# The last chunk of two feed-forward blocks, computed by halves of the tokens

## The chip, the cores and the metric

The kernel runs on one core of one Trainium2 chip. The metric is the time of one execution on the device in microseconds (us); lower is better. The engines named here: PE is TensorE (matrix products; its weight loads are recorded apart as PEld), DVE is VectorE, ACT is ScalarE, POOL is GpSimd, SP issues the transfers. Every engine runs its own program in order and waits on semaphores that the others raise.

## What is computed

Two transformer-like blocks follow each other on 1024 tokens of width 1024. The change touches the ends of their two feed-forward parts, "f" in the first block and "g" in the second:

```python
    u = causal_dwconv(h @ w_up, dw_w) + dw_b            # f
    gt, v = jnp.split(u, 2, axis=-1)
    return (jax.nn.silu(gt) * v) @ w_down
...
        x = x + gt_f * rmsnorm(y, norm_post_ffn[i])     # end of the first block: x2
...
        h = modulate(rmsnorm_2(x, g_mix_pre[layer]), sh1, sc1)
        proj = h @ w_in[layer]                          # first product of the second block
...
        f = swiglu(hf, w_ffn_gate[layer], w_ffn_up[layer], w_ffn_down[layer])   # g
        x = x + g2 * rmsnorm_2(f, g_ffn_post[layer])
    return x
```

`rmsnorm` divides each token by the root of the mean of its 1024 squares. So the residual sum of a token needs the squares of all its 1024 values of y, and the next norm needs the squares of its residual sum.

## The kernel before

Everything lies transposed: channels on the 128 partitions, in 8 tiles of channels (`ND = 8`), and the 1024 tokens along the free dimension. An fp32 product is made of three passes in fp32r: the weight is split into a high and a low part (`wh` cast by ACT in line 1235, `wl` = raw - wh by DVE in line 1713), the activations likewise, and hi·hi, hi·lo and lo·hi are added in PSUM. A PSUM tile ("acc") is 128 x 1024, two banks of 512 tokens; `product` (line 696, matmuls in line 708) issues for each of the three passes one matmul of 512 tokens for each bank, each with its own weight load.

A feed-forward block has 22 tiles of hidden channels. They are gone through in chunks (`CHUNKS`, one of 2 and five of 4). For every chunk `ffn` makes the up products of its hidden tiles and then 8 down products ("dn", chunk, i), one for each output tile i; DVE adds each to the output y(i) in line 1972 ("yadd"). In the last chunk (`LAST`), the down product of tile i is 4 x 3 x 2 = 24 matmuls. After each yadd of the last chunk ACT squares y(i) (line 1284). In f the squares of tile i go straight to PE as the stationary side of small products with one or two columns (`tile_squares`, line 811) that sum over channels, and DVE multiplies y(i) with the stream x(i) (line 1817) and sums these products in `st` (line 1824). In g DVE sums the squares in `st` (line 1976), and PE sums that over channels (line 787). These column sums stand ahead of the last quarter of the next tile's product.

At the end of f `block_end` runs: ACT takes the root, DVE the reciprocal (line 1779) and five small operations that give the mean square of the new stream without having it (lines 1851 to 1860), a second root and reciprocal follow. PE spreads both reciprocals over the 128 partitions (`spread`, line 796, 8 products of 128 x 128 each). ACT copies the first spread from PSUM to `st` (line 1320). Then DVE walks over the 8 tiles with four operations each, in this order: scaled(i) (line 1876), lower(i-1) (line 1896), summed(i), the residual (line 1882), normed(i) (line 1889); ACT makes the high part of the normed tile (line 1325), DVE the low part (lower). PE consumes each tile at once for three weight tiles of `w_in` abreast (`tiles_abreast`, line 754), 3 x 3 x 2 = 18 matmuls a tile. SP stores the new stream x2.

At the end of g, the end of the program, `residual` is the same without the next norm: DVE scales (line 1917) and adds (line 1922), POOL takes the adds of tiles 1, 3 and 5 (line 2518), and SP stores each tile of 128 x 1024.

The order on each engine is the order in which the program of that engine is written out; nothing is scheduled by a tool. Rings (`Ring`) hand out PSUM tiles, temporaries and weight slots in turn: 4 raw weight slots and 3 split ones.

## Time and profile before

| | us |
|---|---|
| median of 3 runs | 3297.73 |
| lowest and highest run | 3294.17, 3299.56 |
| the profiled execution | 3292.07 |
| its span in the trace | 3290.3 |
| PE busy | 3096.4 (94%) |
| DVE busy | 1712.3 (52%) |
| ACT busy | 1011.6 (31%) |
| TensorE clock granted, mean | 0.962 of full speed |

The profiled execution is one execution apart from the three timed ones. Its span lies 1.8 us inside its own time. Times in the trace run from the span's start: the last chunk of f and the block's end lie at 1319 to 1441 us, those of g at 3211 us to the end. The page gives each group of instructions by line, engine and tile, and what ended the idle time before it; the timeline gives the instructions in order of time, neighbours of one kind merged.

### The profile page before, as it was taken

To read this page: it belongs to the slowest core of one execution; us is meant where nothing else is said; L and a number is where in the kernel's file an instruction comes from. 1 tells how busy PE (TensorE), PEld (TensorE's weight loads), DVE (VectorE), ACT (ScalarE), POOL (GpSimd) and SP (SyncE) were. 2 spreads that over 40 slices of the span, in tenths; PEclk is the share of its full clock that TensorE was granted. 3 is DMA by queue.
4 is the path that set the end of the run, shared out by engine and by line. 5 is a ranking of instruction groups with operands and counts; after the bars stand their busy time and mean duration, and the time that the engine had idled before them with its cause. 6 is when DMAs were issued, how large, how long until landed. Compare 5 with 4: busy or idle time off the path is not lost. (4 is left out here: it accounts for less than half of the span.)

```text
span 3290.3 us, 33491 instructions
## 1 busy us (share of the span) xinstructions
PE 3096.4 (94%) x13786; PEld 2499.5 (76%) x13786; DVE 1712.3 (52%) x1776; ACT 1011.6 (31%) x1203; POOL 399.8 (12%) x161
## 2 busy tenths in 40 slices
PE   7998869899999999989999999899999999999996
PEld 3784357788888888778888877677877788888885
DVE  5697786656556554574511076577455322223225
ACT  3454444332222122233221133476222311111111
POOL 0595550000000000000200034000110000000000
PEclk9998879899999999899999999999998999999998
DMA  6114423132223331321432343531331202112112
GB/s 207 58 33 159 148 96 113 73 109 64 90 77 116 100 100 63 109 77 64 141 113 92 108 154 128 136 74 50 126 118 56 76 26 64 49 38 62 38 45 109
DMA packets 96192, 301.24 MB, mean 92 GB/s; under 512 B 11205, under 2 KB 15045, under 8 KB 95847
## 3 DMA queue, kind: packets, MB, share of 16 engines
q1 hardware_dynamic: 96040, 299.09, 27.8%
q8 instruction: 110, 1.80, 0.2%
q14 instruction: 42, 0.34, 0.0%
HBM read 251.34 MB, written 47.71 MB: 91 GB/s over the span
## 5 line engine op out<-in xcount | busy, mean ns | idle before, releaser
L708 PE MATMUL ps<-mainr,wh 128*128 128x512 f32 (+1 forms) x6592 | 1782.0, 390 | 29.5 <-issue 12.7
L708 PEld LDWEIGHTS ps<-mainr,wh 128*128 128x128 f32 x6592 | 1238.6, 189 | 286.6 <-issue 31.2
L708 PE MATMUL ps<-mainr,wl 128*128 128x512 f32 (+1 forms) x3296 | 1030.7, 389 | 0.0
L708 PEld LDWEIGHTS ps<-mainr,wl 128*128 128x128 f32 x3296 | 623.1, 189 | 128.6
L1713 DVE TENSOR_TENSOR wl<-raw,wh 128x1024 fp32r<-128x1024 f32 (+2 forms) x272 | 294.1, 1083 | 457.1 <-ACT wh L1235 456.9
L1235 ACT CAST wh<-raw 128x1024 fp32r<-128x1024 f32 (+2 forms) x320 | 282.0, 886 | 746.9 <-PE ps L708 538.3
L1972 DVE TENSOR_TENSOR mainf<-mainf,ps 128x1024 f32<-128x1024 f32 x80 | 97.7, 1221 | 215.0 <-PE ps L708 215.0
L754 PE MATMUL ps<-mainr,wh 128*128 128x512 f32 x576 | 164.4, 409 | 36.0 <-issue 21.8
L2013 DVE SCALAR_TENSOR_TENSOR ps<-mainf,vec,ps 128x1024 f32<-128x1024 f32 (+1 forms) x174 | 180.9, 1102 | 2.5 <-ACT ps L1424 2.3
L2497 POOL TENSOR_TENSOR tmp<-tmp,mainf 128x1024 f32<-128x1024 f32 x8 | 27.5, 3444 | 1160.6 <-DMA mainf<-in_rope 1097.5
L1049 PE MATMUL ps<-mainr,wh 128*128 128x512 f32 x512 | 160.3, 395 | 6.3 <-POOL wl L2464 6.1
L2464 POOL TENSOR_TENSOR wl<-raw,wh 128x1024 fp32r<-128x1024 f32 x48 | 114.7, 2400 | 421.3 <-ACT wh L1235 421.3
L754 PEld LDWEIGHTS ps<-mainr,wh 128*128 128x128 f32 x576 | 112.3, 198 | 66.6 <-issue 37.8
L1357 ACT CAST mainr<-tmp 128x1024 fp32r<-128x1024 f32 x44 | 46.2, 1050 | 281.7 <-DVE tmp L1951 215.2
L1936 DVE SCALAR_TENSOR_TENSOR tmp<-ps,vec,tmp 128x1023 f32<-128x1023 f32 x44 | 56.3, 1280 | 137.2 <-ACT tmp L1340 137.1
L1951 DVE TENSOR_TENSOR tmp<-ps,tmp 128x1024 f32<-128x1024 f32 x22 | 26.9, 1225 | 184.7 <-PE ps L708 183.6
L1049 PEld LDWEIGHTS ps<-mainr,wh 128*128 128x128 f32 x512 | 97.0, 190 | 27.5 <-issue 6.9
L2355 DVE TENSOR_REDUCE cols<-ps 128x1 f32<-128x1280 f32 x64 | 95.1, 1487 | 43.6 <-PE ps L1114 43.5
L1114 PE MATMUL ps<-mainr 128*128 128x512 f32 (+1 forms) x384 | 98.4, 396 | 15.4 <-DMA mainr<-sc_k 8.2
L2518 POOL TENSOR_TENSOR mainf<-mainf,mainf 128x1024 f32<-128x1024 f32 x3 | 7.0, 2344 | 864.5 <-DVE mainf L1917 864.5
L1340 ACT ACTIVATE tmp<-ps,vec 128x1024 f32<-128x1024 f32 x44 | 52.9, 1205 | 179.6 <-PE ps L708 179.6
L2477 POOL TENSOR_TENSOR mainf<-mainf,mainf 128x1024 f32<-128x1024 f32 x40 | 100.3, 2506 | 34.1 <-ACT mainf L1436 17.5
(236 smaller groups left out, 2896.8 us busy)
## 6 DMA issues: line engine op xcount, KB each, us to landing
raw<-in_mod_w SPq DMA_DIRECT2D x48, 512.0 KB, 4.5
raw<-in_ada_w SPq DMA_DIRECT2D x48, 512.0 KB, 3.7
raw<-in_f_up SPq DMA_DIRECT2D x44, 512.0 KB, 4.2
raw<-in_g_up SPq DMA_DIRECT2D x44, 512.0 KB, 3.5
raw<-in_w_in SPq DMA_DIRECT2D x40, 512.0 KB, 4.1
raw<-in_pw SPq DMA_DIRECT2D x24, 512.0 KB, 3.6
sc_x<-mainf SPq DMA_DIRECT2D x24, 512.0 KB, 2.6
mainf<-sc_x SPq DMA_DIRECT2D x24, 512.0 KB, 6.2
```

The source lines that it names most:

```text
L708: ins = e.matmul(out, wt[:, a:b], xs[n], start=kk == 0 and t == 0, stop=kk == kt - 1 and t == 2)
L754: ins = e.matmul(out, wt[:, a:b], xs[n], start=kk == 0 and t == 0, stop=kk == kt - 1 and t == 2)
L1049: ins = e.matmul(out, wt[:, a:a + 128], x, start=first and t == 0, stop=last and t == 2)
L1114: ins = e.matmul(k.SC[i][:, a:b], k.q_at[u % 3][:, 128 * qt:128 * qt + 128], k.k_at[u % 3][t][:, a:b], start=t == 0, stop=t == 1)
L1235: e.copy(k.WH(j), k.RAWT(j)).then_inc(*k.to("whi", j))
L1713: e.tensor_tensor(k.WL(j), k.RAWT(j), k.WH(j).bitcast(F32), ALU.subtract).then_inc(*k.to("wlo_dve", j))
L1936: e.scalar_tensor_tensor(out=t[:, 1:T], in0=ps[:, 0:T - 1], scalar=k.V("fdw", 3 * f + 1), in1=t[:, 1:T], op0=ALU.mult, op1=ALU.add).then_i ...
L1972: e.tensor_tensor(y(i), y(i), k.ACC(s + "_dn", c, i), ALU.add).then_inc(*k.to("yadd", s, c, i))
L2013: e.scalar_tensor_tensor(out=out[:, a:b], in0=k.U(i)[:, tap + a:tap + b], scalar=k.V("dww", TAPS * i + tap), in1=k.CVP(i)[:, a:b], op0=ALU ...
L2355: e.tensor_reduce(k.STAT(n, i), k.SC[i], AX.X, ALU.max, negate=True).then_inc(*k.to("atmax", n, i))
L2464: e.tensor_tensor(k.WL(j), k.RAWT(j), k.WH(j).bitcast(F32), ALU.subtract).then_inc(*k.to("wlo_pool", j))
L2477: e.tensor_tensor(k.CV(i), k.CV(i), k.PROD(added), ALU.add).then_inc(*k.to("gadd", i, tap))
```

## The change

The last chunk leaves `ffn` and gets a sequence of its own, `last_steps`, which all engines follow. Each down product of the last chunk is now made for 512 tokens at a time, h = 0 or 1: ("dn", i, h) is 12 matmuls into one PSUM bank. The order is (0,0), (0,1), (1,0), (1,1), then half 0 of tiles 2 to 7, then half 1 of tiles 2 to 7. The down weights of two tiles form one weight tile ("dp", p) of 1024 columns. The column sums, the root and reciprocal ("cols"), the spread of the first reciprocal ("res"), of the second ("norm", f alone) and the walk ("pass", i, h) are steps of that sequence for each half. All operations of the walk are 512 tokens wide. In f the first pass stands behind "cols" of half 1; in g passes stand between the last products. In f `scaled` now always reads the copy in `st`, which ACT makes in its step "res". POOL's adds in g go to DVE, the output is stored by halves, and the root's table load on ACT moves ahead of the last chunk. In f x2 is stored when half 1 of a tile is done.

```diff
-        for i in range(ND):
+        for i in range(ND if c < LAST else 0):
             yield ("dn", c, i)
+def last_steps(s):
+    first = [("dn", i, h) for i in range(2) for h in range(2)] + [("dn", i, 0) for i in range(2, ND)]
+    if s == "f":
+        return (first + [("dn", 2, 1), ("dn", 3, 1), ("cols", 0), ("dn", 4, 1), ("res", 0), ("dn", 5, 1), ("norm", 0),
+                         ("dn", 6, 1), ("dn", 7, 1), ("cols", 1), ("pass", 0, 0), ("res", 1), ("pass", 1, 0), ("norm", 1)]
+                + [("pass", i, 0) for i in range(2, ND)] + [("pass", i, 1) for i in range(ND)])
+    return (first + [("dn", 2, 1), ("dn", 3, 1), ("cols", 0), ("dn", 4, 1), ("res", 0), ("dn", 5, 1), ("pass", 0, 0),
+                     ("dn", 6, 1), ("pass", 1, 0), ("pass", 2, 0), ("dn", 7, 1), ("pass", 3, 0), ("pass", 4, 0), ("cols", 1),
+                     ("pass", 5, 0), ("res", 1), ("pass", 6, 0), ("pass", 7, 0)] + [("pass", i, 1) for i in range(ND)])
+def half_before(s, i, h):
+    halves = [step[1:] for step in last_steps(s) if step[0] == "dn"]
+    n = halves.index((i, h))
+    return halves[n - 1] if n else None
...
+    def half_ahead(self, s, i, h):
+        key = {(0, 0): (s + "_dp", 2), (2, 0): (s + "_dp", 3)}.get((i, h))
+        if s in NEXT and (i, h) in ((4, 1), (6, 1)):
+            key = NEXT[s][1][i // 2 - 2]
+        return self.W[key] + 1 if key else 0
...
+        w.wait_ge(*k.at("xyadd", s, ND - 2, h))
+        half_columns(k.S(1)[:, 512 * h:512 * h + 512], k.YC(h, 8), 1, m.ones[:, 0:1], False, False, "x" + s, 0, h)
+        w.wait_ge(*k.at("xy", s, ND - 1, h))
+        half_columns(k.TMP("xy", s, ND - 1, h), k.YC(h, 8), 1, m.ones[:, 0:1], False, False, "x" + s, 1, h)
+        half_squares(s, ND - 1, h)
...
+    def last_chunk(s, slots, lo_hi=None):
+        fs = CHUNKS[LAST]
+        for step in last_steps(s):
+            what, h = step[0], step[-1]
+            a, b = 512 * h, 512 * h + 512
+            if what == "dn":
+                i = step[1]
+                j = k.W[s + "_dp", i // 2]
+                before = half_before(s, i, h)
+                hold_weight(j)
+                hold_half(s + "_dn", i, h)
+                x = lambda kk: ([k.R(slots[0][fs[kk] % 5])[:, a:b]], [k.R(slots[1][fs[kk] % 5])[:, a:b]])
+                sums = s == "f" and before and before[0] < ND - 1
+                product(j, len(fs), x, lambda kk: [("uhi", s, fs[kk]), ("ulo", s, fs[kk])], [k.HALF(s + "_dn", i, h)],
+                        512 * (i % 2), (lambda: half_squares(s, *before)) if sums else None).then_inc(*k.to(*k.half_tile(s, i, h)))
+            elif what == "cols":
+                half_sums(s, h)
+            elif what == "res":
+                hold_half("res", s, h)
+                half_spread("y" + s, h, k.HALF("res", s, h), k.COL("rs", 0, 8))
+            elif what == "norm":
+                n = NEXT[s][0]
+                hold_aux("spread", n, h, banks=(h,))
+                half_spread(n, h, aux[:, a:b], k.COL("rn", 0, 8))
...
+                n, keys = NEXT[s]
+                kk = step[1]
+                w.wait_ge(*k.at("prehi", n, kk, h))
+                w.wait_ge(*k.at("prelo", n, kk, h))
...
+    def last_chunk(s, out, acc_free, hi=None, shift=None, after=()):
+        n = NEXT[s][0] if s in NEXT else None
+        e.activation(k.COL("dum", ("f", "g").index(s)), m.eps[RMS_EPS], ACT.Sqrt)
+        for step in last_steps(s):
+            what, h = step[0], step[-1]
+            a, b = 512 * h, 512 * h + 512
+            if what == "dn":
+                i = step[1]
+                split_to(k.half_ahead(s, i, h))
+                w.wait_ge(*k.at("yadd", s, LAST, i, h))
...
+                e.activation(dst, out(i)[:, a:b], ACT.Square).then_inc(*k.to("ysq", s, i, h))
+            elif what == "cols":
+                if n and h:
+                    split_to(k.W[NEXT[s][1][2]] + 1)
...
+                e.activation(k.COL("rs", 4 * h, 4), src, ACT.Sqrt, bias=m.eps[RMS_EPS]).then_inc(*k.to("sqrt", "y" + s, h))
+            elif what == "res" and n:
+                w.wait_ge(*k.at("stat", s, 4, h))
+                e.activation(k.COL("rn", 4 * h, 4), k.COL("xx", 4 * h, 4), ACT.Sqrt, bias=m.eps[RMS_EPS]).then_inc(*k.to("sqrt", n, h))
+                w.wait_ge(*k.at("spread", "y" + s, h))
+                for event in acc_free:
+                    w.wait_ge(*k.at(*event))
+                e.copy(k.S(0)[:, a:b], k.HALF("res", s, h)).then_inc(*k.to("rcopy", s, h))
+            elif what == "pass" and n:
+                i = step[1]
+                w.wait_ge(*k.at("premul", n, i, h))
...
+                e.activation(hi(i)[:, a:b], k.TMP("pre", n, i, h)[:, 0:512], ACT.Identity, bias=shift(i)).then_inc(*k.to("prehi", n, i, h))
+        if n:
+            split_to(k.W[NEXT[s][1][2]] + 2)
...
+            elif what == "res" and n:
+                rn = k.COL("rn", 4 * h, 4)
+                w.wait_ge(*k.at("sqrt", n, h))
+                e.reciprocal(rn, rn).then_inc(*k.to("rec", n, h))
+            elif what == "pass":
+                i = step[1]
+                xs = x(i)[:, a:b]
+                scaled(i, h, a, b)
+                if n and i:
+                    lower(i - 1, h, a, b)
+                w.wait_ge(*k.at("rmul", s, i, h))
+                w.wait_ge(*k.at(f"x{i}", x_load))
+                e.tensor_tensor(xs, xs, y(i)[:, a:b], ALU.add).then_inc(*k.to("res", s, i, h))
+                if n:
...
+                    hold_tmp("pre", n, i, h)
+                    e.scalar_tensor_tensor(out=k.TMP("pre", n, i, h)[:, 0:512], in0=xs, scalar=k.COL("gm", i), in1=aux[:, a:b],
+                                           op0=ALU.mult, op1=ALU.mult).then_inc(*k.to("premul", n, i, h))
+                    if i == ND - 1:
+                        lower(i, h, a, b)
...
-    for i in (1, 3, 5):
-        w.wait_ge(*k.at("rmul", "g", i))
-        w.wait_ge(*k.at(f"x{i}", "x3"))
-        e.tensor_tensor(k.F(10 + i), k.F(10 + i), k.F(i), ALU.add).then_inc(*k.to("resp", "g", i))
...
+    def last_chunk(s, load, x, key):
+        w.wait_ge(*k.at("tile", k.W[s + "_up", FF - 1, 1]))
+        for p in range(ND // 2):
+            feed(k.W[s + "_dp", p] + RAW)
+            load(2 * p)
+            load(2 * p + 1)
+        if s in NEXT:
+            feed(k.W[NEXT[s][1][2]] + 1 + RAW)
+        for step in last_steps(s):
+            if step[0] != "pass" or (s in NEXT and step[2] == 0):
+                continue
+            _, i, h = step
+            w.wait_ge(*k.at("res", s, i, h))
+            channel(f"st{i}")
+            if s in NEXT:
+                e.dma_start(d[key][i], x(i)).then_inc(*k.land(f"st{i}", key))
+            else:
+                a, b = 512 * h, 512 * h + 512
+                e.dma_start(d[key][i][:, a:b], x(i)[:, a:b]).then_inc(*k.land(f"st{i}", key, h))
```

What now stands in a row on ACT at the end of f (`st<-ps` is the copy of the first spread, `mainr<-tmp` the high part of a normed tile, `wh<-raw` the cast of the third `w_in` weight tile, `cols` the roots). Before:

```order
L1235 CAST wh<-raw 128x1024 [waits s_tile,s_raw2]
L1260 ACTIVATE cols<-ps,cols 128x8 [waits s_cols]
L1316 ACTIVATE cols<-cols 128x8 [waits s_ends_dve]
L1320 COPY st<-ps 128x1024 [waits s_rmul]
L1325 ACTIVATE mainr_24576_51<-tmp,cols 128x1024 [waits s_premul] x8
```

and of the changed kernel, half 1:

```order
L1361 CAST wh<-raw 128x1024 [waits s_tile,s_raw2]
L1516 ACTIVATE cols<-ps,cols 128x4 [waits s_cols]
L1529 ACTIVATE mainr_24576_51<-tmp,cols 128x512 [waits s_premul]
L1519 ACTIVATE cols<-cols 128x4 [waits s_ends_dve]
L1523 COPY st<-ps 128x512 [waits s_spread]
L1529 ACTIVATE mainr_24576_51<-tmp,cols 128x512 [waits s_premul] x15
```

The high part of the first normed half tile now stands ahead of the second root and of the copy of half 1, and the other fifteen behind them.

PE at the same place, behind the last column sums. Before (line 796 the two spreads, 754 the products with `w_in`):

```order
L796 MATMUL ps<-ident,cols 128x128 [waits s_rec,s_yadd]
L796 MATMUL ps<-ident,cols 128x128 x7
L796 MATMUL ps<-ident,cols 128x128 [waits s_ends_dve,s_rec,s_sqrt]
L796 MATMUL ps<-ident,cols 128x128 x7
L754 MATMUL ps<-mainr_24576_51,wh 128x512 [waits s_wlo_dve,s_whi,s_yadd,s_prelo,s_prehi]
```

and of the changed kernel (line 1025 the products with `w_in`, 917 a spread of half 1):

```order
L1025 MATMUL ps<-mainr_24576_51,wh 128x512 [waits s_wlo_dve,s_whi,s_yadd,s_prelo,s_prehi]
L1025 MATMUL ps<-mainr_8192_61,wh 128x512
L1025 MATMUL ps<-mainr_24576_51,wl 128x512
L1025 MATMUL ps<-mainr_24576_51,wh 128x512 [waits s_yadd,s_wlo_dve,s_whi]
L1025 MATMUL ps<-mainr_8192_61,wh 128x512
L1025 MATMUL ps<-mainr_24576_51,wl 128x512
L1025 MATMUL ps<-mainr_24576_51,wh 128x512 [waits s_wlo_dve,s_whi]
L1025 MATMUL ps<-mainr_8192_61,wh 128x512
L1025 MATMUL ps<-mainr_24576_51,wl 128x512
L917 MATMUL ps<-ident,cols 128x128 [waits s_rec]
L917 MATMUL ps<-ident,cols 128x128 x3
L1025 MATMUL ps<-mainr_24576_51,wh 128x512 [waits s_prelo,s_prehi]
```

The spread that ACT's copy waits for now stands behind nine products that need the first normed half tile.

DVE at the end of g of the changed kernel, from the add of the sixth tile's second half (line 2104 yadd, 2110 the sum of squares, 2085 scaled, 2160 the residual, 2133 the reciprocal):

```order
L2104 TENSOR_TENSOR mainf_8192_57<-mainf_8192_57,ps 128x512 [waits s_tile]
L2110 TENSOR_TENSOR st<-st,tmp 128x512 [waits s_yacc,s_ysq]
L2085 SCALAR_TENSOR_TENSOR mainf_8192_57<-mainf_8192_57,cols,ps 128x512 [waits s_spread,s_gain,s_yadd]
L2160 TENSOR_TENSOR mainf_16384_58<-mainf_16384_58,mainf_8192_57 128x512 [waits s_x0,s_rmul]
L2104 TENSOR_TENSOR mainf_8192_57<-mainf_8192_57,ps 128x512 [waits s_tile]
L2110 TENSOR_TENSOR st<-st,tmp 128x512 [waits s_yacc,s_ysq]
L2085 SCALAR_TENSOR_TENSOR mainf_8192_57<-mainf_8192_57,cols,ps 128x512 [waits s_yadd]
L2160 TENSOR_TENSOR mainf_16384_58<-mainf_16384_58,mainf_8192_57 128x512 [waits s_x1,s_rmul]
L2085 SCALAR_TENSOR_TENSOR mainf_8192_57<-mainf_8192_57,cols,ps 128x512 [waits s_yadd]
L2160 TENSOR_TENSOR mainf_16384_58<-mainf_16384_58,mainf_8192_57 128x512 [waits s_x2,s_rmul]
L2104 TENSOR_TENSOR mainf_8192_57<-mainf_8192_57,ps 128x512 [waits s_tile]
```

Five of the sixteen passes stand ahead of the reciprocal of half 1, three of these ahead of the last yadd; two more stand between that reciprocal's spread and the passes of half 1.

## Rows read from the trace of the kernel before

**Rows 1.** The page, part 1: busy us, share of the span, instructions.

```profile
PE 3096.4 (94%) x13786; PEld 2499.5 (76%) x13786; DVE 1712.3 (52%) x1776; ACT 1011.6 (31%) x1203; POOL 399.8 (12%) x161
```

**Rows 2.** Timeline of PE, first tile of f's last chunk: start, us, what [idle <-releaser].

```profile
1326.81 1.25 PE L708 MATMUL ps<-mainr,wh 128*128 128x512 f32 x4 [3.61 <-DVE mainr L1960]
1333.97 1.84 PE L811 MATMUL ps<-cols,tmp 128*128 128x2 f32 x16
```

**Rows 3.** Timeline of PE, end of f, from the last down product on.

```profile
1382.20 0.90 PE L708 MATMUL ps<-mainr,wl 128*128 128x512 f32 x2
1385.51 3.57 PE L811 MATMUL ps<-cols,tmp 128*128 128x2 f32 x16 [2.40 <-ACT tmp L1284]
1392.35 5.56 PE L796 MATMUL ps<-ident,cols 128*128 128x128 f32 x32
1402.61 1.84 PE L754 MATMUL ps<-mainr,wh 128*128 128x512 f32 x4 [4.70 <-issue]
```

**Rows 4.** Timeline of DVE, end of f: the two reciprocals and the walk.

```profile
1389.41 0.20 DVE L1779 RECIPROCAL cols<-cols 128x8 f32<-128x8 f32 x1 [0.26 <-ACT cols L1260]
...
1393.75 0.20 DVE L1779 RECIPROCAL cols<-cols 128x8 f32<-128x8 f32 x1 [0.37 <-ACT cols L1316]
1396.15 1.28 DVE L1876 SCALAR_TENSOR_TENSOR mainf<-mainf,cols,ps 128x1024 f32<-128x1024 f32 x1 [2.20 <-PE ps L796]
...
1401.22 1.28 DVE L1896 SCALAR_TENSOR_TENSOR mainr<-tmp,cols,mainr 128x1024 fp32r<-128x1024 f32 x1
...
1403.68 1.28 DVE L1889 SCALAR_TENSOR_TENSOR tmp<-mainf,cols,ps 128x1024 f32<-128x1024 f32 x1
...
1406.18 1.28 DVE L1896 SCALAR_TENSOR_TENSOR mainr<-tmp,cols,mainr 128x1024 fp32r<-128x1024 f32 x1
...
1435.93 1.28 DVE L1896 SCALAR_TENSOR_TENSOR mainr<-tmp,cols,mainr 128x1024 fp32r<-128x1024 f32 x1 [1.22 <-ACT mainr L1325]
```

**Rows 5.** Timeline of ACT: a high part, and the first work behind the walk.

```profile
1404.99 1.15 ACT L1325 ACTIVATE mainr<-tmp,cols 128x1024 fp32r<-128x1024 f32 x1 [3.81 <-DVE tmp L1889]
...
1439.08 1.05 ACT L1235 CAST wh<-raw 128x1024 fp32r<-128x1024 f32 x1 [3.18 <-PE ps L754]
```

**Rows 6.** Groups by form, 512 tokens wide: busy us, mean ns of one.

```profile
L2013 DVE SCALAR_TENSOR_TENSOR ps<-mainf,vec,ps 128x512 f32<-128x512 f32 x58 | 38.5, 748 | 2.3 <-ACT ps L1424 2.3
L2077 DVE TENSOR_TENSOR tmp<-tmp,ps 128x512 f32<-128x512 f32 x16 | 10.9, 680 | 15.3 <-ACT tmp L1390 15.0 <-DMA sc_H<-tmp 0.3
L1235 ACT CAST wh<-raw 128x512 fp32r<-128x512 f32 x96 | 58.9, 618 | 257.0 <-PE ps L708 252.6 <-PE ps L1049 4.4
```

**Rows 7.** A window: us, busy of PE, PEld, DVE, ACT, POOL, granted clock, DMA share, GB/s.

```profile
2035.00:2040.00 5.00, 3.28 (x19) 2.40 (x18) 1.29 (x2) 2.27 (x4) 2.37 (x1) 1.00 0.00 0
```

**Rows 8.** Timeline of PE, end of g.

```profile
3252.13 1.07 PE L708 MATMUL ps<-mainr,wh 128*128 128x512 f32 x4
...
3253.49 1.84 PE L787 MATMUL ps<-ones,st 128*128 128x1 f32 x16
...
3256.22 0.62 PE L708 MATMUL ps<-mainr,wl 128*128 128x512 f32 x2
3259.24 3.19 PE L787 MATMUL ps<-ones,tmp 128*128 128x1 f32 x16 [2.40 <-ACT tmp L1284]
```

**Rows 9.** Timeline of DVE, end of g.

```profile
3266.80 1.28 DVE L1917 SCALAR_TENSOR_TENSOR mainf<-mainf,cols,ps 128x1024 f32<-128x1024 f32 x1 [3.83 <-PE ps L796]
...
3269.26 2.47 DVE L1917 SCALAR_TENSOR_TENSOR mainf<-mainf,cols,ps 128x1024 f32<-128x1024 f32 x2
...
3284.66 1.22 DVE L1922 TENSOR_TENSOR mainf<-mainf,mainf 128x1024 f32<-128x1024 f32 x1
```

**Rows 10.** Timeline of DVE, the last hidden tile of g.

```profile
3211.60 1.23 DVE L1951 TENSOR_TENSOR tmp<-ps,tmp 128x1024 f32<-128x1024 f32 x1 [9.55 <-PE ps L708]
3213.95 1.23 DVE L1960 TENSOR_TENSOR mainr<-tmp,mainr 128x1024 fp32r<-128x1024 f32 x1 [1.12 <-ACT mainr L1357]
```

**Rows 11.** The page, part 6: x count, KB each, median us to landing.

```profile
out<-mainf SPq DMA_DIRECT2D x8, 512.0 KB, 2.6
```

309 lines of the change are left out of this document (209 added, 100 removed).

## The prediction

> **What bounds the kernel now.** The page comes first: PE is busy for 94% of the span and DVE for 52% [rows 1], so over most of the span PE sets the pace, and a change can pay only where PE waits. I then went to the timelines of PE and DVE at the two places that the change touches.
>
> At the end of f the last down product ends at 1382.20 + 0.90 = 1383.10, and the first product with w_in starts at 1402.61 [rows 3]. Between them PE only makes column sums and spreads, with gaps of 2.40 and 4.70 us. DVE starts its walk over the 8 tiles at 1396.15, 13.05 us behind the last product, and ends it at 1435.93 + 1.28 = 1437.21, after 41.06 us [rows 4]. One tile takes 1406.18 - 1401.22 = 4.96 us there. PE needs only 18 matmuls for a tile. Six matmuls take 3253.49 - 3252.13 = 1.36 us [rows 8], 0.227 us each, so 4.08 us a tile: DVE sets the pace of the walk. The next work hangs on the first w_in tile, which ACT picks up at 1439.08 [rows 5].
>
> At the end of g nothing follows. The last product ends at 3256.22 + 0.62 = 3256.84 [rows 8], DVE's last add at 3284.66 + 1.22 = 3285.88 [rows 9]; then comes the last store.
>
> **The end of f, from its start.** What goes away is the wait of half 0 for the sums of half 1. I count four terms: until the last down product, from there to the walk, the walk, and what hangs on it.
>
> First term, PE until the last down product. The last chunk's first tile needs the last hidden tile only for its fourth quarter, and PE already waits 3.61 us for it [rows 2]. Before, 18 matmuls (4.08 us) of that tile cover the wait. Now the first product has 12 matmuls, nine ahead of that quarter (2.04 us), so the wait grows by 2.04 us. The 192 matmuls of the chunk stay 192, each already with its own weight load. Column sums of a whole tile are 16 records in 1.84 us [rows 2], 0.115 each; of a half 8 in 0.92. The squares cost the same in sum. Before, one set of 1.84 (the stream's products) stood ahead of the last product's end; now three sets for half 0 do, 2.76: +0.92. Two spreads of half 0, 8 records each, come between the products too: at 0.12 each 0.96, at the mean of the 32 before (5.56 us, [rows 3]) 1.39. I take the first, since PE is busy there and the 32 began behind a gap: +1.92 (to +2.8). Sum +4.9: the last product ends at 1388.0.
>
> Second term. DVE adds 512 tokens in 0.68 us and multiplies them with the stream in 0.75 [rows 6]: with the hand-overs 1.54. PE sums that product (0.92, at 2.5) and the squares (at 3.4). The root takes 0.3, the reciprocal 0.2 [rows 4], the five small operations I take like it, 1.0 together. The walk can start 5.0 us behind the last product, not 13.05: -8.05. It no longer waits for a spread, since half 0's were made long before. The cast and the low part of the third w_in weight (1.05 on ACT [rows 5] and about 1.2 on DVE) lie beside the column sums. If PE runs at the low clock there, where 16 records took 3.57 us [rows 3], 1.8 us come on top; its gap is now only 0.6 us, so I take none.
>
> Third term, the walk itself. None of its 16 passes stands ahead of the last product: the first is behind "cols" of half 1. So the walk is not beside the products at all in f, it only begins earlier, and it is made of twice as many instructions. A half saves 0.53 us (1.28 against 0.748, 1.22 against 0.680, [rows 4, 6]), not half of it. From lower to lower DVE needs 1403.68 - 1401.22 = 2.46 to normed, less two times 0.53, 1.40; normed 0.75; then ACT's high part, 1.15 [rows 5] less what the cast saves (1.05 - 0.618 = 0.43, [rows 5, 6]), 0.72; hand-overs 0.07. That is 2.94 us a pass, 15 times from the first lower to the last, 44.1. With 3.07 ahead of the first, 0.77 for the last and 0.8 for the change of halves (the high part of tile 7 has nothing beside it) the walk is 48.75 us against 41.06: +7.7.
>
> On top come two waits that the order makes. ACT and PE go through "pass (0,0)" ahead of "res (1)". DVE ends normed(0) 2.3 us into the walk, at 7.3 behind the last product. ACT makes the high part (8.0), then the second root (8.3), for which DVE waits with its reciprocal ahead of pass (1,0): about 1.0 lost. Then lower(0) ends at 9.8. PE makes the nine products of pass (0,0) first. It has waited 6 us by then; behind a gap of 4.70 four matmuls took 1.84 [rows 3], and nine at 0.43 take 3.9, until 13.7. The spread follows, 0.96 to 1.8 (14.7 to 15.5), ACT's copy 0.6, and only then ACT makes the high part of tile 1 (16.1 to 16.9), which lower(1) needs, 12.0 without this. DVE waits 4.4 us. If PE were at full speed at once, nine take 2.04 and the wait is 2.2. Queued behind ACT's waiting copy are fifteen high parts, behind PE's spread all products with w_in. I take 5.4 for both waits, bounds 3.2 and 6.4.
>
> Fourth term. Behind the last lower the first w_in tile needs three matmuls, not six: -0.7. PE then waits for what ACT and DVE make of it, as before. SP stores x2 only with half 1, issued as the tiles are done, and the last store follows the last add as it did; its readers come more than 10 us later. SP's loads of the stream stand ahead of the down products and stay early. These I cost at nothing.
>
> The sum for f: 4.9 - 8.05 + 7.7 + 5.4 - 0.7 = **+9.25 us**, bounds +6 and +13.
>
> **The end of g.** The low part of the last hidden tile is ready at 3213.95 + 1.23 = 3215.2, the down products start as DVE's line 1951 does, at 3211.6 [rows 10]. Before, the fourth quarter is reached at 3215.7, without a wait; now at 3213.6: +1.6. The column sums inside the products stay 1.84, a spread of 0.96 is added: the last product ends at 3259.4 (a wait that short leaves the clock up: in the window 2035 to 2040, PE busy 3.28 of 5 us, it stayed at 1.00 [rows 7]).
>
> On DVE a half product costs yadd 0.68, the wait for ACT's square (0.62, as the cast of [rows 6]) and the sum 0.68: 2.1 with hand-overs, inside the 2.72 of PE. A pass is scaled and add: 3269.26 - 3266.80 = 2.46 [rows 9] less 1.07, 1.39. From the end of product (5,1), 5.44 ahead of the last: 2.1 and one pass, yadd (6,1) starts at 3.4 where its product ended at 2.7; 2.1 and two passes, yadd (7,1) at 8.2 instead of 5.5. From here DVE is the bound. Two passes cover the square, the column sums and the root of half 1 (11.6), the reciprocal 0.2, eleven passes 15.3: 27.2, or 21.8 behind the last product, 3281.2. POOL's three adds are now in these passes; before they saved DVE 3 x 1.14. Against 3285.88 that is **-4.7 us**. The last store, 2.6 us for 512 KB [rows 11], may be some tenths shorter with half the bytes; I take none. Bounds: -6 with that and a shorter first wait, -2.5 if the clock falls for the first products as it did in f.
>
> **Sum.** +9.25 - 4.7 = +4.6 us. The profiled execution took 3292.07, 1.8 over its span, and lies 5.7 under the median; I add the sum to the median: 3297.73 + 4.6 = **3302.3**. What a measurement here can tell from no change is about 0.2%, 6.6 us: 3291.1 to 3304.3.
>
> **The rivals.**
>
> *The low clock in the walk (slower).* PE gets 9 matmuls (2.04 us) for every 2.94 us of DVE. If the clock once fallen stays at 1.2 GHz, nine take 3.9, PE becomes the bound of the walk: 15 x 0.95 = 14.3 more, 3316.6. It decides as soon as nine matmuls need over 2.94. Against it: the window of [rows 7] held 1.00 at a busy share of 66% with gaps, and at low clock the nine fill PE wholly, the state in which it has risen elsewhere. The Trainium skill, "TensorE: Matmul & The Clock Gate", section "HAM oscillation — how this bites in real kernels", describes a kernel whose bursts of matmuls were shorter than the waits between them and which started every burst at the low clock; by that rule this rival would need waits longer than the bursts, and they are shorter here. Chance 0.12.
>
> *Halves at half price (faster, a little).* If a pass of 512 took half of 4.96, 2.48, f would save 7.4 and g's thirteen passes 2: 3292.9. Against it stand the rows of 512-wide operations. Chance 0.08.
>
> *The change does what its name says in f.* If DVE made half 0's passes beside the products of half 1, some 23 us of the walk would be hidden: about 3279. The order of DVE excludes it, the first pass is behind the second "cols". Chance 0.04.
>
> *Something else waits*, such as a ring slot or a weight among the halves, 3 us or more in either block: 3306 and up. Chance 0.08.
>
> **How the numbers follow.** The forecast has 0.68, its own range 3297 to 3308, since its bounds add to -0.5 to +10 and its waits are the soft terms; some 0.50 of it lie under 3304.3, 0.18 above. Faster by over 0.2%: 0.04 of the third and 0.03 of the second rival, 0.07. Slower: 0.18 + 0.12 + 0.06 = 0.36. Within: 0.57. The range runs from the second rival to beyond the fourth, 3293 to 3312.
>
> **What would show it.** In f: PE's wait ahead of the first tile's last quarter near 5.6 us; the first scaled 5 us behind the last product; one lower of DVE waiting 4 us for ACT, and ACT's copy waiting for a spread behind nine slow matmuls; lowers 2.94 apart; the walk over 50 us long. In g: a wait of 1.6 in the first product, no idle DVE from yadd (6,1) on, the last add 22 us behind the last product. It would be wrong if PE's clock stays at 0.50 through the walk, if lowers stand 2.5 apart, or if DVE idles between passes in g.

## The result

The changed kernel takes 3301.3 us (median of 17 runs, 3293.6 to 3309.4), the kernel before 3294.5 us (17 runs, 3287.7 to 3300.4). The ratio is 1.0021, 95% interval 1.0015 to 1.0028: slower by 5 to 9 us, some 7 at the middle. The forecast was 3302.3 us, 4.6 us above the median that it started from.

The profiled execution took 3307.02 us with a span of 3305.2, 14.9 us more than the profiled one of before. Part 1 of the page of the changed kernel:

```profile
PE 3105.4 (94%) x13786; PEld 2500.9 (76%) x13786; DVE 1724.8 (52%) x1863; ACT 1017.2 (31%) x1223; POOL 392.8 (12%) x158
```

Against [rows 1] PE has 9.0 us more and DVE 12.5; the shares are the same. The 14.9 us can't all be the change. To see where they lie I took five events that both programs have and compared the stretches between them: DVE's multiply of f's last hidden tile, ACT's cast behind the walk [rows 5], a table load of ACT in the second block, DVE's multiply of g's last hidden tile [rows 10], DVE's last add [rows 9]. Timelines of the kernel before, DVE and ACT, the two events that no row ahead has:

```profile
1323.10 1.23 DVE L1946 TENSOR_TENSOR tmp<-tmp 128x1024 f32<-128x1024 f32 x1
...
2081.33 1.28 ACT L1645 ACT_TABLE_LOAD   x1
```

The five events in the changed kernel, timelines of DVE and ACT:

```profile
1329.44 1.23 DVE L2195 TENSOR_TENSOR tmp<-tmp 128x1024 f32<-128x1024 f32 x1
...
1454.87 1.05 ACT L1361 CAST wh<-raw 128x1024 fp32r<-128x1024 f32 x1 [1.95 <-PE ps L1025]
...
2097.80 1.28 ACT L1810 ACT_TABLE_LOAD   x1
...
3231.53 1.23 DVE L2200 TENSOR_TENSOR tmp<-ps,tmp 128x1024 f32<-128x1024 f32 x1 [8.59 <-PE ps L771]
...
3300.77 0.69 DVE L2160 TENSOR_TENSOR mainf<-mainf,mainf 128x512 f32<-128x512 f32 x1
```

| stretch, us | before | after | difference |
|---|---|---|---|
| start to f's last hidden tile | 1323.10 | 1329.44 | +6.34 |
| **f**: from there to the cast behind the walk | 115.98 | 125.43 | **+9.45** |
| to the table load | 642.25 | 642.93 | +0.68 |
| to g's last hidden tile | 1130.27 | 1133.73 | +3.46 |
| **g**: from there to the end of the last add | 74.28 | 69.93 | **-4.35** |
| to the span's end | 4.42 | 3.74 | -0.68 |

The change touches the f and g stretches and the last store: +9.45 - 4.35 - 0.68 = +4.4 us, where the prediction's sum was +4.55. The other 10.5 us stand where both programs issue the same; the same kernel run again (e9) shows that these differ between executions. The lower end of the measured interval is +4.9 us, above these +4.4. Where the rest lies is not shown: over all kernels below, the stretch behind the walk alone comes out between 640.0 and 643.0 us, so its +0.68 can't be told from chance.

**f, the first product.** Timeline of PE of the changed kernel (start, us, what, idle before and releaser):

```profile
1324.85 0.61 PE L771 MATMUL ps<-mainr,wl 128*128 128x512 f32 x2
1329.55 1.19 PE L771 MATMUL ps<-mainr,wh 128*128 128x512 f32 x2 [4.09 <-issue]
```

and of DVE, the read of the last up tile and the low part of the hidden tile:

```profile
1328.06 1.28 DVE L2188 SCALAR_TENSOR_TENSOR tmp<-ps,vec,tmp 128x1022 f32<-128x1022 f32 x1
...
1331.78 1.23 DVE L2209 TENSOR_TENSOR mainr<-tmp,mainr 128x1024 fp32r<-128x1024 f32 x1 [1.11 <-ACT mainr L1483]
```

PE waits, but not ahead of the fourth quarter, as in [rows 2] and as predicted: it waits 4.09 us ahead of the whole first half product, until DVE has read the last up tile out of PSUM (1328.06 + 1.28 = 1329.34; the row itself only says "issue", e5 below shows that it is the bank). The half banks begin with the bank in which that tile lies. The fourth quarter is not far off as a second bound. In another execution of the same kernel (e9) the first matmuls still ran at full clock, two in 0.70 instead of 1.19 us, and PE then waited for the low part too:

```profile
1323.90 0.70 PE L793 MATMUL ps<-mainr,wh 128*128 128x512 f32 x2 [4.09 <-issue]
...
1327.50 1.16 PE L793 MATMUL ps<-mainr,wh 128*128 128x512 f32 x2 [0.46 <-DVE mainr L2281]
```

In both executions the first column sums start 7.4 us behind DVE's multiply.

**f, from the last product to the walk.** Timelines of the changed kernel, PE from the last down product on:

```profile
1393.15 0.40 PE L771 MATMUL ps<-mainr,wl 128*128 128x512 f32 x1
...
1395.11 1.36 PE L887 MATMUL ps<-ones,tmp 128*128 128x1 f32 x8 [0.78 <-DVE tmp L2122]
1396.33 1.85 PE L887 MATMUL ps<-cols,tmp 128*128 128x2 f32 x8
1404.40 1.19 PE L1025 MATMUL ps<-mainr,wh 128*128 128x512 f32 x2 [6.22 <-issue]
...
1408.37 1.52 PE L917 MATMUL ps<-ident,cols 128*128 128x128 f32 x8
```

ACT:

```profile
1409.93 0.59 ACT L1523 COPY st<-ps 128x512 f32<-128x512 f32 x1 [7.15 <-PE ps L917]
```

DVE, the first scaled, the second reciprocal and three of the sixteen lowers:

```profile
1399.59 0.74 DVE L2085 SCALAR_TENSOR_TENSOR mainf<-mainf,cols,st 128x512 f32<-128x512 f32 x1
...
1402.82 0.18 DVE L2151 RECIPROCAL cols<-cols 128x4 f32<-128x4 f32 x1 [0.98 <-ACT cols L1519]
...
1411.17 0.75 DVE L2092 SCALAR_TENSOR_TENSOR mainr<-tmp,cols,mainr 128x512 fp32r<-128x512 f32 x1 [4.83 <-ACT mainr L1529]
...
1414.10 0.75 DVE L2092 SCALAR_TENSOR_TENSOR mainr<-tmp,cols,mainr 128x512 fp32r<-128x512 f32 x1
...
1452.95 0.75 DVE L2092 SCALAR_TENSOR_TENSOR mainr<-tmp,cols,mainr 128x512 fp32r<-128x512 f32 x1 [0.79 <-ACT mainr L1529]
```

The whole chain that was forecast is here. Nine matmuls at the low clock (granted clock 0.50 from 1396 on) take 1408.37 - 1404.40 = 3.97 us, the spread stands behind them, ACT's copy waits 7.15 us for the spread, the second high part waits for the copy, and DVE's second lower waits 4.83 us for that. Lowers then stand 2.93 us apart (1414.10 - 1411.17).

**g.** Timelines of the changed kernel, DVE's reciprocal of half 1:

```profile
3286.09 0.18 DVE L2133 RECIPROCAL cols<-cols 128x4 f32<-128x4 f32 x1 [0.15 <-ACT cols L1516]
```

and PE's first wait and last product:

```profile
3232.97 0.70 PE L771 MATMUL ps<-mainr,wh 128*128 128x512 f32 x2 [1.54 <-issue]
...
3279.37 0.39 PE L771 MATMUL ps<-mainr,wl 128*128 128x512 f32 x1
```

From the end of the last product, 3279.76, to the last add's end, 3301.46, are 21.70 us (before 29.04 [rows 8, 9]). From yadd (6,1) on DVE idles only once for ACT's square (0.70 us) and these 0.15 us.

### The profile page after: what moved, and what is told of

Same layout as the page of the kernel before. It is cut to its first block and busy times, and to the rows that moved or that the text cites. A ratio compares the mean times of both kernels' runs of the same rounds, so it can differ in the third digit from the quotient of the medians.

```text
span 3305.2 us, 33621 instructions
## 1 busy us (share of the span) xinstructions
PE 3105.4 (94%) x13786; PEld 2500.9 (76%) x13786; DVE 1724.8 (52%) x1863; ACT 1017.2 (31%) x1223; POOL 392.8 (12%) x158
## 5 line engine op out<-in xcount | busy, mean ns | idle before, releaser
L771 PEld LDWEIGHTS ps<-mainr,wh 128*128 128x128 f32 x6592 | 1238.5, 189 | 289.2 <-issue 34.4
L771 PE MATMUL ps<-mainr,wl 128*128 128x512 f32 (+1 forms) x3296 | 1041.5, 389 | 0.0
L2219 DVE TENSOR_TENSOR mainf<-mainf,ps 128x1024 f32<-128x1024 f32 x64 | 78.1, 1221 | 176.9 <-PE ps L771 176.9
L1176 PE MATMUL ps<-mainr,wh 128*128 128x512 f32 x512 | 161.7, 397 | 6.1 <-POOL wl L2702 6.1
L817 PE MATMUL ps<-mainr,wh 128*128 128x512 f32 x480 | 137.7, 411 | 28.4 <-issue 17.2
L817 PEld LDWEIGHTS ps<-mainr,wh 128*128 128x128 f32 x480 | 94.3, 199 | 53.1 <-issue 27.7
L1176 PEld LDWEIGHTS ps<-mainr,wh 128*128 128x128 f32 x512 | 98.1, 192 | 27.5 <-issue 6.9
L2715 POOL TENSOR_TENSOR mainf<-mainf,mainf 128x1024 f32<-128x1024 f32 x40 | 100.3, 2507 | 34.2 <-ACT mainf L1600 17.7
L1176 PE MATMUL ps<-mainr,wl 128*128 128x512 f32 x256 | 101.5, 396 | 0.0
```

The source lines that it names most:

```text
L771: ins = e.matmul(out, wt[:, a:b], xs[n], start=kk == 0 and t == 0, stop=kk == kt - 1 and t == 2)
L817: ins = e.matmul(out, wt[:, a:b], xs[n], start=kk == 0 and t == 0, stop=kk == kt - 1 and t == 2)
L1176: ins = e.matmul(out, wt[:, a:a + 128], x, start=first and t == 0, stop=last and t == 2)
L2219: e.tensor_tensor(y(i), y(i), k.ACC(s + "_dn", c, i), ALU.add).then_inc(*k.to("yadd", s, c, i))
L2715: e.tensor_tensor(k.CV(i), k.CV(i), k.PROD(added), ALU.add).then_inc(*k.to("gadd", i, tap))
```

## The experiments

Each experiment was run 7 to 12 times beside the kernel before on the same chip. The table has what each gave; "f" and "g" are the stretches defined above, of one profiled execution each.

| kernel | ratio to before, 95% | f | g | start to f | table load to g |
|---|---|---|---|---|---|
| before | 1 | 115.98 | 74.28 | 1323.1 | 1130.3 |
| the change | 1.0021 (1.0015 to 1.0028) | 125.43 | 69.93 | 1329.4 | 1133.7 |
| e9 the change again | 1.0016 (1.0005 to 1.0028) | 125.41 | 69.93 | 1323.8 | 1130.1 |
| e1 g alone | 0.9989 (0.9980 to 0.9998) | 115.82 | 69.89 | 1327.9 | 1131.3 |
| e2 f alone | 1.0028 (1.0017 to 1.0039) | 125.41 | 74.20 | 1324.1 | 1130.1 |
| e3 f reordered | 0.9990 (0.9981 to 0.9999) | 120.43 | 69.91 | 1324.2 | 1126.8 |
| e4 f beside products | 0.9991 (0.9981 to 1.0000) | 118.44 | 69.91 | 1322.3 | 1130.1 |
| e7 the same, casts ahead | 0.9988 (0.9978 to 0.9997) | 114.94 | 69.92 | 1325.7 | 1130.9 |
| e5 ring of banks | 1.0019 (1.0009 to 1.0028) | 128.00 | 69.93 | 1323.9 | 1127.2 |
| e6 quarters abreast | 1.0024 (1.0015 to 1.0034) | 128.83 | 67.87 | 1323.7 | 1133.7 |
| e8 POOL's adds in g | 1.0020 (1.0011 to 1.0030) | 125.44 | 69.26 | 1324.7 | 1130.6 |
| e10 whole tiles in f | 0.9990 (0.9981 to 0.9999) | 115.06 | 69.90 | 1327.4 | 1126.6 |
| **e11 e10 + quarters in g** | **0.9984 (0.9975 to 0.9993)** | 115.20 | 67.86 | 1322.6 | 1126.8 |
| e12 e7 earlier + quarters in g | 0.9986 (0.9976 to 0.9996) | 115.16 | 67.86 | 1328.7 | 1126.9 |

The medians resolve less than the stretches. A kernel's difference of medians from the kernel before and the sum of its differences in f, g and behind the last add lie up to 3.2 us apart (from -2.1 in e3 to +3.2 in e12). So the ratios tell faster from slower, and the stretches tell why, to some tenths.

### One place at a time: e1, e2, e9

The halves are kept for one block and the old path is taken for the other.

```diff
+HALVED = ("g",)        # e2: ("f",), e9: ("f", "g")
...
-        for i in range(ND if c < LAST else 0):
+        for i in range(ND if c < LAST or s not in HALVED else 0):
...
```

e9 has both blocks in `HALVED` and so issues what the changed kernel issues.

> The halves at the end of g alone; f as in the kernel before. My theory (the sum of the prediction, term of g -4.7 us; between the two profiled executions the end of g is 4.35 us shorter behind the same work): 3294.5 - 4.7 = 3289.8 us, a ratio of 0.9986 (0.998 to 0.9992). The rival: the profiled execution of the changed kernel stands 6.35 us late ahead of f's last chunk already and gains another 4.1 us between the end of f and the last chunk of g, where the program is the same; if that comes with the program (its code or its semaphores) and not with the execution, this kernel is not faster, ratio 1.000 or above.

> The halves at the end of f alone; g as in the kernel before. My theory: +9.25 us by the sum, +9.4 by the two traces (the cast behind the walk at 1454.87 against 1439.08, less the 6.35 us by which the traces differ ahead of the place): ratio 1.0028, between 1.0024 and 1.0036. If the two ends are independent, its difference and that of the kernel with g alone add up to the +6.8 us of the whole change. The rival in which f costs nothing or little and the loss is elsewhere: ratio under 1.001.

> The changed kernel once more, instruction for instruction. The stretches of its program are to be compared between two profiled executions: my theory is that f (multiply of the last hidden tile to the cast behind the walk) takes 125.4 us again and g (multiply of the last hidden tile to the last add) 69.9, while the 1329.44 us ahead of f and the 1133.7 us between the score stage's table load and g, which the change does not touch, come out differently by some us; ratio to the kernel before 1.0021 (1.001 to 1.003). The rival: they come out at 1329 and 1134 again, so the change costs time there too.

g alone is faster: 3290.9 against 3293.9 us. f alone is slower: 3303.0 against 3293.9. The medians are -3.0 and +9.1 us, together +6.1; the change has +6.8. The stretches are those of the changed kernel and of before to 0.2 us: each block's end does what it does whatever the other does. The same kernel again has its f and g stretches to 0.02 us, but stands 5.6 us earlier ahead of f. Timelines of that run, DVE and ACT:

```profile
1323.79 1.23 DVE L2267 TENSOR_TENSOR tmp<-tmp 128x1024 f32<-128x1024 f32 x1
...
1449.20 1.05 ACT L1410 CAST wh<-raw 128x1024 fp32r<-128x1024 f32 x1 [1.96 <-PE ps L1065]
```

So the rival (time lost in untouched places) falls: ahead of f the same kernel differs from itself by 5.6 us, between the table load and g by 3.7, and over all kernels each of these two stretches varies by up to 7 us (last two columns of the table). Part of it can be TensorE's clock: in the windows 2100 to 2200 of before and of the changed kernel the granted clock stood at 0.97 and 0.93 (columns as in [rows 7]); why it differs was not traced. Before:

```profile
2100.00:2200.00 100.00, 89.91 (x498) 76.01 (x497) 75.00 (x96) 68.47 (x116) 0.00 (x0) 0.97 0.37 81
```

The changed kernel:

```profile
2100.00:2200.00 100.00, 85.99 (x458) 72.68 (x456) 76.43 (x99) 67.50 (x112) 0.00 (x0) 0.93 0.33 73
```

### The two waits in the walk: e3

```diff
-                         ("dn", 6, 1), ("dn", 7, 1), ("cols", 1), ("pass", 0, 0), ("res", 1), ("pass", 1, 0), ("norm", 1)]
-                + [("pass", i, 0) for i in range(2, ND)] + [("pass", i, 1) for i in range(ND)])
+                         ("dn", 6, 1), ("dn", 7, 1), ("cols", 1), ("res", 1), ("norm", 1)]
+                + [("pass", i, h) for h in range(2) for i in range(ND)])
```

> The whole change, but in f the second root, both spreads and ACT's copy of half 1 stand ahead of the first pass of half 0 instead of between the first passes. My theory: the two waits of 0.98 and 4.83 us in the walk go, and about 1 us comes on top ahead of the walk (second root 0.3, reciprocal 0.2 and their hand-overs): -4.8 us against the changed kernel, so +2 us against the kernel before, ratio 1.0006 (1.000 to 1.0012); in the trace the first scaled 7 us behind the last product, lowers 2.9 apart from the first on, walk of 48 to 49 us. The rival: the 4.83 us were due to the low clock of PE or to ACT, and a wait of that size appears at another place of the walk: ratio 1.002 as the changed kernel.

Timeline of DVE:

```profile
1394.87 0.18 DVE L2151 RECIPROCAL cols<-cols 128x4 f32<-128x4 f32 x1 [0.36 <-ACT cols L1519]
1394.97 0.72 DVE L2085 SCALAR_TENSOR_TENSOR mainf<-mainf,cols,st 128x512 f32<-128x512 f32 x1
...
1397.98 0.75 DVE L2092 SCALAR_TENSOR_TENSOR mainr<-tmp,cols,mainr 128x512 fp32r<-128x512 f32 x1
...
1400.91 0.75 DVE L2092 SCALAR_TENSOR_TENSOR mainr<-tmp,cols,mainr 128x512 fp32r<-128x512 f32 x1
...
1442.69 0.75 DVE L2092 SCALAR_TENSOR_TENSOR mainr<-tmp,cols,mainr 128x512 fp32r<-128x512 f32 x1 [0.79 <-ACT mainr L1529]
```

Both waits are gone, the walk takes 1443.44 - 1394.97 = 48.5 us instead of 54.1, and f 5.0 us less, as expected. The wait of 4.83 us was the order on ACT and PE. The measured ratio, 0.9990, lies below the 1.000 to 1.0012 that I expected. About half of the miss is that I took the 4.8 us off the median difference of 6.8 and not off the 4.4 of the traces. By the stretches the kernel is 0.6 us faster than before (+4.45 - 4.37 - 0.64), a ratio of 0.9998, inside the measured interval; nothing in the trace shows more.

### Passes beside the products: e4, e7, e12

e4 gives PE its products with `w_in` as steps of their own and puts three passes of half 0 between the last three down products and two more ahead of the last column sums; e7 has ACT cast the second and third `w_in` weights ahead of high parts and puts the last lower of half 0 behind the first scaled of half 1; e12 makes the spread and the first passes one product earlier (the cast of the second weight moves with them) and has e6's order in g.

```diff
+                         ("pass", 0, 0), ("dn", 6, 1), ("pass", 1, 0), ("pass", 2, 0), ("dn", 7, 1),
+                         ("pass", 3, 0), ("pass", 4, 0), ("cols", 1), ("mul", 0, 0), ("pass", 5, 0), ("res", 1), ("norm", 1),
+                         ("mul", 1, 0), ("pass", 6, 0), ("mul", 2, 0), ("pass", 7, 0)] + [("mul", i, 0) for i in range(3, ND)]
+                + [(what, i, 1) for i in range(ND) for what in ("pass", "mul")])
```

> The whole change, but in f the vector and scalar work of the first five passes of half 0 stands between the last three down products of half 1 (as in g), PE's products with w_in of these passes behind the last down product. My theory: DVE is the bound from the norm of half 0 on. From there it has two products' work (2 x 2.16) and 16 passes of 2.94, 51.4 us, and 1.5 of small operations; 7.4 us of it lie ahead of the end of the last down product, so the walk ends 45.5 us behind that product, where the changed kernel has 6.0 + 54.1 = 60.1: -14.6 us against it, -8 us against the kernel before, ratio 0.9977 (0.996 to 0.9985). Rival 1: PE becomes the bound behind the last product, since all 144 products with w_in now follow it (32.7 us at full clock, 61 us at the low clock): if the clock stays low, ratio 1.000 or above. Rival 2: yadds that come late block PE's banks and the last product comes late by as much as is hidden: ratio 1.002.

> As the kernel with the passes of half 0 beside the down products in f, but ACT casts the second and third w_in weights ahead of the high parts behind which they queued, and the low part of tile 7 of half 0 stands behind the scaling of tile 0 of half 1. The stretch of f was 118.4 us there, not 110.8 as I expected; in its trace DVE waits 1.73 and 1.72 us for these casts, makes two low parts of weights of 1.23 us that I had not counted, waits 0.79 us at the change of halves and 0.98 us for the second root, and PE's last product is 2.3 us late. My theory: two casts 3.45 us, the change of halves 0.8, and up to 1 us that PE no longer waits: the stretch 118.4 - 4.3 = 114.1 us (113 to 115), ratio to the kernel before 0.9975. The rival: DVE's waits were only time in which it waited for PE's column sums anyway; then the stretch stays above 117 us.

> As the kernel with the passes of half 0 beside the down products in f and the casts ahead of the high parts (stretch of f 114.94 us), with the second spread and the first pass of half 0 one down product earlier, where DVE was idle 2.27 us; and the quarters' order in g (67.87 us). My theory: DVE starts its passes some 4 us earlier, of which 2.3 us was idle time: f 112.7 us (111.5 to 114), g 67.9 us, -3.3 - 6.4 - 0.7 = -10.4 us against the kernel before, ratio 0.9968. The rival: PE is the bound of this stretch by now (144 products with w_in behind the last sums, the first of them at the low clock), and f stays at 114 us or above.

e4 took 7.0 us off f, not 14.6. Timeline of DVE of e4:

```profile
1384.34 1.23 DVE L1878 TENSOR_TENSOR wl<-raw,wh 128x1024 fp32r<-128x1024 f32 x1 [1.73 <-ACT wh L1364]
...
1402.05 1.23 DVE L1878 TENSOR_TENSOR wl<-raw,wh 128x1024 fp32r<-128x1024 f32 x1 [1.72 <-ACT wh L1364]
```

and of PE:

```profile
1394.75 1.87 PE L890 MATMUL ps<-ones,tmp 128*128 128x1 f32 x8 [4.37 <-DVE tmp L2122]
```

I had left out the two low parts of weights (1.23 us each) that DVE makes there, and the casts that queue behind high parts on ACT; DVE waits 1.73 and 1.72 us for these, and PE 4.37 us for DVE ahead of the last column sums. With the casts ahead (e7) f is 114.94, near the 114.1 expected, 10.5 us under the changed kernel; the ratio, 0.9988, is above the 0.9975 expected, for the stretches give 6.0 us against before and the medians 3.2. e12 started the passes earlier still and brought nothing: f 115.16, not 112.7. Windows of e12 (PE busy, PEld, DVE, ACT, POOL, granted clock, DMA share, GB/s):

```profile
1420.00:1430.00 10.00, 10.00 (x46) 8.29 (x45) 9.37 (x14) 2.75 (x4) 0.00 (x0) 1.00 0.51 204
1430.00:1440.00 10.00, 10.00 (x46) 8.29 (x45) 9.46 (x15) 2.17 (x3) 0.00 (x0) 1.00 0.40 159
```

PE is busy without a gap at full clock: the rival held. All 144 products with `w_in` now follow the last column sums, and from 1413 on they are the bound. But DVE's own walk did not end earlier either: the last lower ends 113.2 us behind the multiply of the last hidden tile, in e7 112.9. DVE made its first pass ahead of a down product's yadd instead of behind it, and then waited 2.40 us for that product, where in e7 it had been idle for 2.27. The product came later, since PE now waits 1.58 us for DVE's second reciprocal ahead of the spread. PE and DVE of e12:

```profile
1382.48 1.13 PE L921 MATMUL ps<-ident,cols 128*128 128x128 f32 x8 [1.58 <-DVE cols L2177]
...
1387.32 0.69 DVE L2130 TENSOR_TENSOR mainf<-mainf,ps 128x512 f32<-128x512 f32 x1 [2.40 <-PE ps L775]
```

So e12 moved the idle time and did not remove it.

### The price of halves: e10

```diff
-                         ("dn", 6, 1), ("dn", 7, 1), ("cols", 1), ("pass", 0, 0), ("res", 1), ("pass", 1, 0), ("norm", 1)]
-                + [("pass", i, 0) for i in range(2, ND)] + [("pass", i, 1) for i in range(ND)])
+                         ("dn", 6, 1), ("dn", 7, 1), ("cols", 1), ("res", 1), ("norm", 1)]
+                + [("pass", i, 1) for i in range(ND)])
...
-                xs = x(i)[:, a:b]
+                if n:
+                    a = 0
+                xs = x(i)[:, a:b]
```

(ACT's high part, DVE's four operations and PE's products with `w_in` then take 1024 tokens.)

> The whole change, but in f the walk goes over whole tiles of 1024 tokens, behind the sums, roots and spreads of both halves; the down products and column sums stay in halves. Tests the third term of the prediction, the price of two half operations against a whole one. My theory: the walk takes 41.1 us as in the kernel before and starts 6.7 us behind the last product (as in the kernel with the second root ahead of the passes) instead of 13.05; the last product is 4.1 us late; so the stretch of f is 115.98 + 4.1 - 6.35 = 113.8 us (113 to 115), 6.7 us less than with half passes in the same order (120.43), and the ratio to the kernel before (-2.2 in f, -4.35 - 0.7 in g) 0.9978. The rival: the halves' walk was slow for another reason (ACT's latency, PE's order), whole tiles bring under 3 us, the stretch stays above 117 us.

Timeline of DVE:

```profile
1399.56 1.28 DVE L2088 SCALAR_TENSOR_TENSOR mainf<-mainf,cols,st 128x1024 f32<-128x1024 f32 x1 [1.32 <-ACT st L1526]
...
1404.64 1.28 DVE L2095 SCALAR_TENSOR_TENSOR mainr<-tmp,cols,mainr 128x1024 fp32r<-128x1024 f32 x1
...
1439.34 1.28 DVE L2095 SCALAR_TENSOR_TENSOR mainr<-tmp,cols,mainr 128x1024 fp32r<-128x1024 f32 x1 [1.22 <-ACT mainr L1532]
```

The walk takes 1440.62 - 1399.56 = 41.06 us, to the hundredth what it took before [rows 4], against 48.5 in halves, also behind both spreads (e3): halves cost 7.4 us, predicted 7.7. f is 115.06, 1.3 us over the estimate, and those are the 1.32 us for which the first scaled waits for ACT's copy.

### The wait ahead of the first product: e5, e6

e5 starts the ring of half banks at the bank that was free longest; e6 also issues quarters 0 to 2 of (0,0) and (0,1) ahead of both fourth quarters.

```diff
-        half.only(*range(6))
+        r = 2 * self.acc.turn[self.acc.next % 3]
+        half.only(*((b + r) % 6 for b in range(6)))
...
+        for h in range(2):
+            hold_half(s + "_dn", 0, h)
+            quarters(h, range(3))
+        for h in range(2):
+            quarters(h, (3,)).then_inc(*k.to(*k.half_tile(s, 0, h)))
```

> The whole change, but the ring of half banks starts at the bank that has been free longest, so that the first down product of the last chunk no longer waits for DVE to read the last up tile. In the trace of the changed kernel PE waits 4.09 us ahead of the whole first product in f (DVE ends the read at 1329.34, PE starts at 1329.55) and 1.54 us in g, not ahead of the fourth quarter as the prediction had it. My theory: this costs nothing, because the low part of the last hidden tile, which the fourth quarter needs, is ready only at 1333.01, and PE reached that quarter at 1333.4; with the bank free the wait moves to the fourth quarter and the product ends within 0.5 us of the same moment. From the multiply of the last hidden tile to the cast behind the walk 125.4 us as in the changed kernel (+-0.5), ratio to the kernel before 1.002. The rival: the bank is what counts, and the span gets shorter by 2 to 4 us in f and up to 1.5 in g; ratio 1.001.

> As the kernel with the ring started at the free bank, and in addition the first three quarters of both halves of the first tile stand ahead of both fourth quarters (the column sums of these two move one product on). My theory: this takes back the 2.04 us of the first term of the prediction, in f with the low clock behind the wait (nine matmuls more are done inside the wait, 2.04 to 3.9 us): the stretch of f 125.4 - 2.5 = 122.9 us, the stretch of g 69.9 - 1.6 = 68.3 us; together -4 us against the changed kernel, ratio 1.0009 (1.000 to 1.0015). The rival: the cover of the wait is not what makes the last product late, and neither stretch gets shorter.

Timeline of PE of e5:

```profile
1327.64 1.19 PE L772 MATMUL ps<-mainr,wh 128*128 128x512 f32 x2 [5.65 <-DVE mainr L2210]
...
1332.50 0.95 PE L888 MATMUL ps<-cols,tmp 128*128 128x2 f32 x8
```

of the changed kernel at the same column sums:

```profile
1336.82 1.02 PE L887 MATMUL ps<-cols,tmp 128*128 128x2 f32 x8
```

and of e6:

```profile
1327.39 0.70 PE L1004 MATMUL ps<-mainr,wh 128*128 128x512 f32 x2 [3.61 <-DVE mainr L2232]
```

e5: the wait moves to the fourth quarter and is 5.65 us, 3.61 + 2.04, just what the prediction had put there. I expected the product to end at the same moment all the same. It ends later: the first column sums start 1332.50 - 1323.93 = 8.57 us behind the multiply of the last hidden tile, in the changed kernel 1336.82 - 1329.44 = 7.38. Twelve matmuls lie between the wait and these sums, and PE makes them in 4.86 us, most of them at the low clock. The changed kernel began its first product 3.6 us earlier, reaches the same twelve 0.4 us later, is soon back at full clock and makes them in 3.29 us. So the bank is not what makes the first product late; waiting for it is even the cheaper wait by 1.2 us.

e6: the wait is 3.61 us again, as before the change, and g loses 2.06 us (expected 1.6). In f too the quarters bring something at first: with 33 matmuls and one set of column sums done, e6 is 9.63 us behind the multiply, the changed kernel 11.10. But f got longer in both. The last down product of f ends 66.80 us behind the multiply in e5 and 67.50 in e6, in the changed kernel 64.11, so both lose time again further on. Windows of e6 (columns as above):

```profile
1364.00:1368.00 4.00, 4.00 (x28) 3.58 (x27) 2.48 (x4) 0.64 (x1) 0.00 (x0) 1.00 0.02 4
1368.00:1372.00 4.00, 4.00 (x22) 3.61 (x22) 1.65 (x4) 1.83 (x3) 0.00 (x0) 0.67 0.01 2
1372.00:1376.00 4.00, 4.00 (x15) 3.52 (x14) 1.83 (x6) 0.00 (x0) 0.00 (x0) 0.50 0.18 38
1376.00:1380.00 4.00, 4.00 (x15) 3.47 (x15) 2.22 (x4) 1.41 (x3) 0.00 (x0) 0.55 0.23 93
```

and of the changed kernel at the same instructions:

```profile
1374.00:1378.00 4.00, 4.00 (x31) 3.76 (x30) 1.57 (x3) 1.61 (x3) 0.00 (x0) 1.00 0.00 0
```

TensorE went to its low clock (0.50, 1.2 GHz) within the column sums of half 0, four sets of 8 records (fp32 matmuls of 1 or 2 columns, two records each) from 1365.50 to 1370.2, although the record shows no gap. The profile models where a matmul ends, so a short idle time between such small ones would not show. As an estimate from the windows, 12 us at 0.67, 0.50 and 0.55 cost 4 x (0.33 + 0.50 + 0.45) = 5.1 us, near the 4.9 that e6 loses there by the count of matmuls; without them f would be 123.7, near the 122.9 expected. In the changed kernel the same four sets left the clock at 1.00. In e5 the fall was shorter (0.87 and 0.70 over 8 us, 1.7 us by the same estimate), and with the 1.2 us at the first product it comes to 2.9, near the 2.6 us by which f is longer. The Trainium skill, "TensorE: Matmul & The Clock Gate", section "HAM oscillation — how this bites in real kernels", ties the fall to waits of PE; a fall without a recorded gap is not what it describes. What decides it was not settled: it was one execution of each, and the changed kernel and e9, the same program, already differ in where the clock falls at the first product. The medians of e5 (+6.0 us) and e6 (+7.6 us) say only that f's quarters bring nothing.

### DVE as the bound of g: e8

```diff
+                if n or not h or i not in (1, 3, 5):
+                    e.tensor_tensor(xs, xs, y(i)[:, a:b], ALU.add).then_inc(*k.to("res", s, i, h))
```

(POOL makes the other three adds, of half 1.)

> The whole change, but POOL takes the adds of tiles 1, 3 and 5 of half 1 in g, as it took whole tiles before. Tests the statement that DVE is the bound at the end of g. My theory: DVE has three adds of 0.69 us less, the stretch from the multiply of the last hidden tile of g to DVE's last add 69.9 - 2.1 = 67.8 us, and the span is as much shorter as long as POOL's add of tile 5 ends ahead of DVE's last; ratio to the kernel before 1.0015. The rival: POOL's adds slow DVE's operations beside them, and the stretch stays at 69 us or above.

Timeline of DVE of e8:

```profile
3283.78 1.52 DVE L2085 SCALAR_TENSOR_TENSOR mainf<-mainf,cols,ps 128x512 f32<-128x512 f32 x2
3285.34 1.08 DVE L2161 TENSOR_TENSOR mainf<-mainf,mainf 128x512 f32<-128x512 f32 x1
```

and of POOL:

```profile
3284.60 1.27 POOL L2756 TENSOR_TENSOR mainf<-mainf,mainf 128x512 f32<-128x512 f32 x1 [861.73 <-DVE mainf L2085]
```

g is 69.26, only 0.67 us shorter and not 2.1: the rival held. POOL's add runs to 3285.87, and DVE's add of two SBUF operands, started at 3285.34, takes 1.08 us instead of 0.69; DVE's scaling, which reads one operand from PSUM, keeps 0.76. Three times 0.39 us takes back over half of the 2.07. The Trainium skill, "SBUF — State Buffer", section "Who interferes with whom", says that a VectorE instruction with two SBUF inputs has to wait while a GpSimd instruction that reads SBUF holds the port that they share, and one with a single SBUF input doesn't. The trace agrees in kind on both; in size the add took 0.39 us longer where POOL's add had 0.53 us still to run (spans on POOL are rough).

### The combination: e11

The diffs of e10 and, for g alone, of e6.

> As the kernel with the walk over whole tiles in f, and in g (not in f) the ring of banks started at the free bank and the first three quarters of both halves of tile 0 ahead of both fourth quarters, which took the stretch of g from 69.93 to 67.87 us. My theory: the two are independent, f 113.8 us, g 67.9 us: -2.2 - 6.4 - 0.7 = -9.3 us against the kernel before, ratio 0.9972 (0.996 to 0.998), faster than both kernels. The rival: TensorE's granted clock falls in the column sums of g when they come 2 us earlier, as it did in f with the same edit, and takes the gain back; then 0.998 or above.

3287.6 against 3293.0 us, ratio 0.9984 (0.9975 to 0.9993): faster than the kernel before by some 5 us, and than the changed kernel by 9 (median of e9 beside it) to 12 us (by the stretches). The stretches are 115.20 and 67.86: -0.78 - 6.42 - 0.65 = -7.9 us against before by the traces, less than the -9.3 expected because of ACT's copy in f. The ratio lies where I had put the rival, above 0.998, but the rival's mechanism is not there: g is 67.86, as in e6. The intervals of the five kernels that are faster than before with f changed (e3, e7, e10, e11, e12) overlap; that e11 is the best of them is not shown.

## Why the prediction was right

By its steps, f measured from DVE's multiply of the last hidden tile, so that the differences ahead of it drop out:

| term | predicted | measured |
|---|---|---|
| last product of f late | +4.9 | +4.1 (64.11 against 60.00) |
| last product to the first scaled | -8.05 | -7.0 (6.04 against 13.05) |
| the walk without its waits | +7.7 | +7.2 (54.11 - 5.81 - 41.06) |
| the two waits in it | +5.4 | +5.8 (0.98 + 4.83) |
| behind the walk | -0.7 | -0.7 (1.17 against 1.87) |
| **f** | **+9.25** | **+9.45** |
| **g** to the last add | **-4.7** | **-4.35** |
| the last store | 0 | -0.7 |

The mechanism holds but for the place of the first wait and the clock at the start of the walk; still, the closeness of the sum is partly luck: the four larger terms of f miss by -0.8, +1.0, -0.5 and +0.4 us and cancel to 0.2, and this and g's miss of 0.35 stand against the 0.7 of the store, which the sum had at nothing.

- *The first product.* The place and the size were wrong. PE stood ahead of the product and not ahead of its fourth quarter, since I had not looked at which bank the first half product takes. With the bank free (e5) PE does wait the predicted 5.65 us at the fourth quarter, so the working was right for a kernel without the wait for the bank. Because PE began the product later, its first matmuls fell into the wait's end and the loss was 4.09 - 3.61 = 0.5 us of idling and 0.6 us more at the low clock (11 matmuls in 4.78 us; before 12 in 4.41), where the sum had 2.04. What is left of the +4.1 are column sums and spreads, 3.0 us against the 2.84 of the sum.
- *The start of the walk.* I took no low clock ahead of it, because PE's gap is short (0.78 us measured, 0.6 predicted). The two column sums took 1.36 and 1.85 us, not 0.92 each; the second is what such a set takes at the low clock. The granted clock was 1.00 ahead of the gap and 0.50 from 1396 on: the clock fell behind even so short a gap, and this is the 1.0 us that the term lacks, inside the 1.8 that I had as the bound.
- *The walk.* Halves at 2.93 us (2.94 predicted); e10 against e3 shows that it is the width. The waits by the order were 5.8 us; e3 took them away.
- *The rival of the low clock.* PE was back at full clock from 1416.6 on and waited 0.6 to 0.7 us for DVE in nearly every pass from 1423.8 on: the rival fell. The rows fit the reasons given (nine matmuls at the low clock filled PE, and its waits are short), no run tests them apart.
- *g.* DVE is the bound from yadd (6,1) on, as forecast, up to 0.15 us. The last add follows the last product by 21.70 us (21.8 predicted); the last product is 3.0 us late (48.23 us behind the multiply against 45.24) where the sum had 2.6, and that is most of the miss of 0.35. e6 shows what the first wait was worth: without it g is 2.06 us shorter, against the 1.6 of the sum.
- *The level.* I added the sum to a median of three runs, 3297.7; over 17 runs the kernel before stands at 3294.5. The forecast of +4.6 us lies just under the interval of the measured difference, +4.9 to +9.2, so the time came out near for the sum and a base 3 us too high. Against the second set of runs of the same kernel (+1.6 to +9.2 us by its ratio) it lies inside.

## What to carry to other kernels

Splitting a reduction by halves pays where the other half's work is really put beside products: here g had this and gained 4 us, f had only the earlier start and paid 7 us for twice as many instructions. Even so the prize in f was small: with half passes beside the products (e7) it came to 114.9 us and with whole tiles behind both halves' sums (e10) to 115.1, either way 1 us under the 116.0 of before. When steps of two halves are interleaved by one list for all engines, follow what each engine queues behind the step: one pass ahead of a spread cost 4.8 us, and the list was the only thing to change. And once the engine that was the bound is relieved, count the next one's whole remaining work: in f PE's 144 products with `w_in` became the bound once DVE's passes stood ahead of the last column sums, and a still earlier start (e12) only moved DVE's idle time.

## What the runs showed of the hardware

- TensorE's granted clock can fall from 1.00 to 0.50 where the record shows PE busy throughout, in a stretch of small column sums (e6, 1366 to 1380), and stay at 1.00 behind the same instructions in another kernel (the changed kernel, 1374 to 1378).
- It also fell to 0.50 among column sums behind a gap of only 0.78 us (the changed kernel, from 1396 on; so too e3, e5, e6, e9 and e10, where the second set behind that gap took 1.63 to 1.85 us instead of 0.95).
- In two executions of one program it fell at different instructions: ahead of f's first half product in the profile of the changed kernel (two matmuls in 1.19 us), within it in e9 (0.70 us).
- The same instructions outside the change took between 1322.3 and 1329.4 us, and between 1126.6 and 1133.7 us, from one profiled execution to the next. A difference of two spans says nothing below some 10 us here; the stretches f and g of one program (the changed kernel and e9) repeated to 0.02 us.
- A DVE add of two SBUF operands took 1.08 us beside an add on POOL and 0.69 alone.
